# A hybrid block followed by an attention block on one Trainium2 core: 256 unused bytes ahead of the shared buffer and a rounded offset inside it

## The reference

```
u = rmsnorm(x) @ w_in                                   # 16 row blocks of 128
x = x + mix @ w_out                                     # mix: the four mixers' outputs
n = rmsnorm(x, ffn_norm)
x = x + (silu(n @ w_gate) * (n @ w_up)) @ w_down        # 2048 -> 5632 -> 2048
proj = rms_norm(x, g) @ w_in_2
merged = g_a * (ya @ w_proj_a) + g_b * (yb @ w_proj_b) + g_m * (ym @ w_proj_m)
x = x + merged @ w_out_2
```

## The kernel before, in words

| tensor | before: start, remainder by 512 | with the change |
|---|---|---|
| `nS` | 16512, 128 | the same |
| `ringH` | 49280, 128 | the same |
| `ringL` | 65664, 128 | the same |
| `AR`, `hS`, `yS`, `gateS` | 125696, 256 | 125952, 0 |
| `SC` | 13904 words | 13952 words |
| `xS` | 181312, 64 | 181760, 0 |

## Time and profile before

### The profile page before, as it was taken

How to read it: one execution, slowest core, us unless ns; L and a number is a source line. 1 busy time by engine, 2 the same in 40 slices (tenths; PEclk the granted TensorE clock), 3 DMA queues, 4 the chain that set the end, 5 groups by cost and what they waited for, 6 DMA issues and landing times.

```text
span 2373.0 us, 31285 instructions
## 1 busy us (share of the span) xinstructions
PE 2346.9 (99%) x12704; PEld 1949.0 (82%) x12704; DVE 1498.0 (63%) x1945; ACT 1129.3 (48%) x1423; POOL 299.2 (13%) x455
## 2 busy tenths in 40 slices
PE   8999999999999999999999999999999999999998
PEld 7777789988888888888888888888888888888887
DVE  6887767787755555555555666655456756555564
ACT  6635446564553444444443464455444455444444
POOL 1100011210011111100111142200004230000000
PEclk9999999999999999999999999999999999999999
DMA  8643355655656666656666567655547665665664
GB/s 302 196 142 109 124 174 192 216 165 204 203 192 201 203 203 194 198 196 202 197 195 202 177 232 242 211 167 176 163 157 224 219 207 185 222 208 193 203 247 142
DMA packets 258543, 461.86 MB, mean 195 GB/s; under 512 B 13408, under 2 KB 78560, under 8 KB 256096
## 3 DMA queue, kind: packets, MB, share of 16 engines
q1 hardware_dynamic: 241984, 423.65, 54.5%
q0 software_dynamic: 15840, 35.68, 4.6%
q10 hardware_dynamic: 576, 0.53, 0.1%
HBM read 435.16 MB, written 14.68 MB: 190 GB/s over the span
## 4 chain that ended last, share of the span: by engine, by line
PE 92%; DVE 5%; ACT 1%; DMA 1%; issue 1%; SPq 0%; ACTq 0%; DVEq 0%
PE pp L708 25%; PE pp L710 25%; PE pp L709 25%; PE pp L737 7%; PE pp L738 3%; DVE ringL L2052 1%; PE ps L665 1%; PE ps L1312 1%; PE ps L1326 1%; PE ps L856 0%; DMA raw<-in_w_in 0%; DMA mem_hold<-memSt 0%; ACT ringH L1400 0%; PE pp L743 0%; PE pp L744 0%
## 5 line engine op out<-in xcount | busy, mean ns | idle before, releaser
L2052 DVE TENSOR_TENSOR ringL<-raw,ringH 128x1024 fp32r<-128x1024 f32 x779 | 961.9, 1242 | 637.4 <-ACT ringH L1400 635.1
L1400 ACT CAST ringH<-raw 128x1024 fp32r<-128x1024 f32 x779 | 814.7, 1050 | 970.0 <-PE pp L710 858.4
L708 PE MATMUL pp<-ringH,nS 128*128 128x512 f32 x1376 | 542.7, 394 | 0.0
L710 PE MATMUL pp<-ringH,nS 128*128 128x512 f32 x1376 | 536.2, 390 | 0.0
L709 PE MATMUL pp<-ringL,nS 128*128 128x512 f32 x1376 | 535.7, 389 | 0.0
L737 PE MATMUL pp<-nS,ringH 128*128 128x512 f32 x992 | 361.8, 406 | 7.0 <-DVE ringL L2046 3.2
L710 PEld LDWEIGHTS pp<-ringH,nS 128*128 128x128 f32 x1376 | 258.3, 188 | 54.1
L708 PEld LDWEIGHTS pp<-ringH,nS 128*128 128x128 f32 x1376 | 258.5, 188 | 53.0 <-issue 0.4
L709 PEld LDWEIGHTS pp<-ringL,nS 128*128 128x128 f32 x1376 | 258.5, 188 | 51.9 <-issue 0.2
L533 POOL DMA_DIRECT2D AR<-AR x304 | 160.7, 550 | 963.6 <-DVE AR L2115 517.8
L738 PE MATMUL pp<-nS,ringL 128*128 128x256 f32 x992 | 278.5, 281 | 0.0
(11 more groups left out here) (414 smaller groups left out, 2038.8 us busy)
## 6 DMA issues: line engine op xcount, KB each, us to landing
raw<-in_w_in SPq DMA_DIRECT2D x189, 1024.0 KB, 5.2
raw<-in_ffn_w_gate SPq DMA_DIRECT2D x44, 1024.0 KB, 5.4
raw<-in_ffn_w_up SPq DMA_DIRECT2D x44, 1024.0 KB, 5.1
raw<-in_ffn_w_down SPq DMA_DIRECT2D x44, 1024.0 KB, 5.0
raw<-in_w_out SPq DMA_DIRECT2D x32, 1024.0 KB, 5.1
raw<-in_w_mem_kv SPq DMA_DIRECT2D x16, 1024.0 KB, 5.4
AR<-AR POOLq DMA_DIRECT2D x304, 32.0 KB, 4.7
raw<-in_w_proj_a SPq DMA_DIRECT2D x8, 1024.0 KB, 5.5
```

The costliest lines, as they stand in the source:

```text
L708: mm(o, XH[:, ts(j)], WH, first, False)
L710: t_of[0] = mm(o, XL[:, ts(j)], WH, False, last)
L1400: e.copy(ringH[:, h % NSPL, 0:nh * cols], raw[:, u % NRAW, h0 * cols:(h0 + nh) * cols]).then_inc(*hi.tick(h))
L2052: tt2(ringL[:, h % NSPL, o], raw[:, u % NRAW, h0 * cols:(h0 + nh) * cols], ringH[:, h % NSPL, o].bitcast(F32), SUB).then_inc(*lo.tick(h))
```

## The change

256 bytes of unused padding are allocated ahead of `AR`, so that `AR` begins on a multiple of 1024 bytes, and `SC` is rounded up to a multiple of 128 words in place of 8. `AR` gets 64 words shorter. Every region of `AR` ahead of `SC` moves by 256 bytes, every region counted from `SC` by 448 bytes, and the ones counted from the end of `AR` stay where they are. No instruction is added, removed or moved on any engine.

```
@@ -348,6 +348,8 @@
         grow = sb("grow", [128, 5, T])
         gcol = sb("gcol", [128, 2, 12])
         w2s = sb("w2s", [128, 512])
+        if nc.sbuf_base % 1024:
+            sb("to_line", [128, (1024 - nc.sbuf_base % 1024) // 4])
         base = nc.sbuf_base
         NAR = ((nc.sbuf_usable_end - base) // 4 - 8) // 8 * 8
         AR = sb("AR", [128, NAR])
@@ -441,7 +443,7 @@
         MVo = MU + 8 * GW
         RU = MVo + 1024
         RW_ = 1 + T
-        SC = (RU + 14 * RW_ + 7) // 8 * 8
+        SC = (RU + 14 * RW_ + 127) // 128 * 128
         mix = v3(MIXo, 16, T)
         gU = v3(GU, 12, GW)
         mU = v3(MU, 8, GW)
```

## The result

The changed kernel takes 2385.61 us (median of 5 runs, 2383.61 to 2387.92), against 2374.99 us for the kernel before in the runs beside it: a ratio of **1.0039**, 95% interval 1.0029 to 1.005. It is slower by 10.6 us where +7.2 were forecast. That is inside the stated range of 2361 to 2388 us, and just outside the narrower one that the prediction calls the forecast's own, 2380 to 2385.

The account below looks back on a forecast made before the run. TensorE, never idle from 640 to 2240 us, was taken as the bound, so pace per matmul counts. +7.2 us on `xS` and 0 elsewhere took 2375.6 to 2382.8 us; range 2361 to 2388, the forecast's own 2380 to 2385.

Parts of the forecast that it names:

- The reading by distance: Dense matmuls: pace follows stationary start minus moving start; 226.7 ns at 0, 228.9 at 64 below, 232.3 at 128 above.
- own alignment: Dense matmuls: the reading that a rounder start of the stationary tensor should be cheaper; rejected since 256 was the dearest remainder.
- 128 below and 128 above are one place: Matmuls on `xS`, `hS`, `yS`: a pattern repeating every 256 bytes would give all three the old pace of `hS`, 232.3 ns.
- `xS`: +7.2 us: 2112 matmuls on `xS`: pace goes from 228.9 to 232.3 ns, adding 7.2 us.
- `hS`: 0: Matmuls on `hS`, summed with `yS` as 1536: pace stays at 232.3 ns, adding 0 us.
- one value for the three: Profile after: distances between starts on `xS`, `hS` and `yS` must be one value; 232.3 ns would confirm the sum.
- The cost rises with the distance in either direction: Dense matmuls: pace grows as the stationary start lies further below or above the moving one, fitting 226.7, 228.9, 232.3 ns.
- Rival 2: Matmuls on `xS`, `hS`, `yS`: cost linear in distance, pace 231.1 ns, +2.8 us, 2378.4 us; chance 0.16.
- The small terms: Small matmuls from `AR` (-1.0 to +1.0 us, taken as 0), `gateS` (0.1 us), and hidden VectorE, ScalarE and DMA accesses.
- The row with 256 moving columns: Matmuls with `gateS` stationary: 118.5 ns at 128 above, against 120.0 at equal remainders; held against distance as a law.
- Rival 1: Matmuls on `xS`, `hS`, `yS`: alignment brings all to the pace of `nS`, -13.2 us, 2362.4 us; chance 0.22.
- Rival 4: Dense matmuls: paces belong to the stages, not the start byte, so nothing changes, 2375.6 us; chance 0.08.

## Why the prediction was right, and where it was off

- **What bounds it**, right. TensorE had no idle time from 640 us on, before and after, and 10.07 us of the 11.6 us between the spans lie in the feed-forward layer alone.
- **The reading by distance**, right, and against own alignment: shown by the kernel with everything on 512 and by the one with the rings moved, in which an operand changes its pace without being moved.
- **"128 below and 128 above are one place"**, right, and by one only of the two forms from which it was taken. The repeat after 256 bytes held; "only the size of the distance counts" did not (228.9 ns at 64 below, 233.4 at 64 above). The padding alone shows it for `hS` (232.3 ns on both sides), and for `xS` with 192 above and 64 below (229.0 and 228.9).
- **`xS`: +7.2 us**, the term that was too small. It was 2112 x 3.4; the pace came to 233.4 ns and not 232.3, so 2112 x 4.5 = 9.5 us (9.1 as added up in the trace). The step that failed was taking the pace of `hS` before as the pace at distance 128. It was the pace of `hS` behind an `xS` at 228.9 ns; `xS` itself took 233.4 at 128 in both kernels that put it there.
- **`hS`: 0**, off by 0.9 us for the same reason: its long block behind small matmuls, and all of `yS`, behind `nS`, kept 232.4 ns, while the nine blocks behind `xS` went to 233.4. So the test "one value for the three" was also wrong as it was put: there were two.
- **"The cost rises with the distance in either direction"**, wrong as a law. Rival 2 and the upper end of the range rest on it. 32 bytes off costs as much as 128. The three values that the trace held happened to lie on a rising line. That the value at 128 came out near the forecast is due to the repeat, not to this law.
- **The small terms**, right: VectorE and ScalarE kept their busy times, and no new wait came.
- **The row with 256 moving columns**, rightly held against distance as a law. There equal remainders take 119.8 to 120.0 ns and other places as little as 117.9.
- **Rival 1**, the gain by alignment, fell, though its number came up elsewhere. It forecast 2362.4 us, the pace of `nS` for all. A kernel with every operand of the dense products on a multiple of 512 takes that (2360.8 and 2362.2 us), but so does one with every operand at remainder 128 (2363.4 and 2361.8), so alignment isn't what brings it. And the change doesn't give the alignment that it was announced with: `nS` and both rings stay at 128.
- **Rival 4**, that the addresses don't matter, fell. The Trainium skill, in TensorE: Matmul & The Clock Gate, section Step-by-step: what each phase is for, gives the streaming and the stationary operand independent ports. The runs don't speak on the ports, but the two streams are not independent in time: the pace depends on the distance of their starts, from 226.7 to 234.3 ns.

What stays open is why. That the pair of start addresses sets the pace is shown from both sides; by what mechanism, why it repeats after 256 bytes, what picks between two paces at distance 128, and why the order of the places is another one with 256 moving columns, no run here shows. None of the eight distances went below 226.7 ns.

## What to carry to other kernels

Where TensorE is full, compare the distance between starts of equal matmuls on different tensors, not their durations: 228.9 against 226.7 ns is invisible in a group's mean and was 0.2% of this kernel on one tensor. Before aligning anything, print the addresses that the allocator gives, of the operands that stay as well, since what counts is the pair: here `xS`, `hS` and `yS` moved onto a round number made the kernel 0.4% slower, and the same tensors moved onto the remainder of their partner made it 0.5% faster. That holds for 512 moving columns; with 256, equal remainders were among the dear places, so measure the form that you have. A small tensor at the front shifts everything behind it, as the 64 bytes ahead of `ringH` did.

## What the runs showed of the hardware that was not expected

- With fp32r operands, a 128x128 stationary tile and 512 moving columns, the distance between starts depends on the two start addresses by 256 bytes: 226.7 ns at equal remainders, 228.9 with the stationary one 64 bytes below, 232.3 to 234.3 at the six other multiples of 32.
- With 256 moving columns the order is another: 119.8 to 120.0 ns at equal remainders, 118.5 with the stationary operand 128 above, 117.9 with it 64 above.
- The same operands can have two steady paces, 232.3 and 233.4 ns at distance 128, and keep them for 96 matmuls and more. For `hS` it went with the matmuls ahead: 232.3 to 232.4 behind an `xS` at 228.9 ns or behind small matmuls, 233.4 behind an `xS` at 233.4.
- A stretch bound by TensorE repeats almost exactly: 722.16 us for 3168 dense matmuls and some small ones, in two executions whose earlier stages differed by 3.1 us.
